# The seam from the first output product to gate-up: high parts first, low parts behind them, and the weight splits placed elsewhere

## The chip, the cores and the metric

The kernel runs on one core of one Trainium2 chip. Its engines are TensorE (PE in the profile, with its weight loads as PEld), VectorE (DVE), ScalarE (ACT), GpSimd (POOL) and SyncE (SP, which here only issues DMA transfers). The metric is the time of one execution in device microseconds. The kernel before took 1119.88 us as the median of three runs (1119.84 to 1121.58).

## The reference

Two transformer blocks on 512 tokens of 1024 features in fp32, one after the other. The change touches the place in the first block where attention ends and the feed-forward part begins:

```python
mixed = concatenate([rms_norm(out_a, group_norm_a), rms_norm(out_b, group_norm_b)], axis=-1) @ w_out
x = x + rms_norm(mixed, norm_mix_post)
h = rms_norm(x, norm_ffn_pre)
f = (silu(h @ w_gate) * (h @ w_up)) @ w_down
```

The product with w_out is called out1 in the kernel, the two products with w_gate and w_up are gate-up (gu1). Each of gate and up has 2816 columns, 22 tiles of 128. The second block has the same parts under the names out2 and gu2.

## The kernel before

**Layout and precision.** Features lie on the 128 partitions and tokens run along the free dimension, so x is eight blocks k of 128 features by 512 tokens (`xres[:, k, :]`). Each fp32 operand of a product is written as a high part in the format fp32r and a low part that holds what is left. A product is three matmuls: high weights by high state, high weights by low state, low weights by high state. The state h has the tiles `hh` (high) and `hl` (low); a chunk of weights, 1024 x 128, has `raw`, `wh` and `wl`, with a ring of four slots for chunks. The weights of gate-up tile j are chunk gu1+j. A split of a chunk is two steps: ACT copies `raw` to `wh` (`act_split`, L460), and DVE subtracts to get `wl` (`vec_split`, L472). ACT's step needs the slot's last tile to be multiplied, and DVE's step releases the load that SP issues into that slot of `raw`.

**Halves.** At this seam the tokens are taken in two halves of 256. The last three tiles of out1 are multiplied for the first half of the tokens and then for the second (units 5 to 7 and 8 to 10). From each half the kernel takes the mean square (ACT squares, DVE adds, PE sums over the partitions with a matrix of ones in `half_sum`, ACT makes `rstd` from it), and then, block by block: DVE scales (`vec_scale`, L1573, into `ta`), DVE adds to x (`vec_update`, L1580), ACT writes the high part of h (`act_half_h`, L1681) and a square for the next norm (L1682), and DVE writes the low part (`vec_half_low`, L1585). `vec_mix` and `vec_mix_add` (L1540, L1547) take a unit of out1 out of the banks, and `vec_half_square` (L1557) adds a square. The norm of h itself is not needed at this point, since its factor is applied to the products later.

**Gate-up's start.** `pe_gu1_first` multiplies the first four tiles of gate-up (two of gate, two of up), one per bank, for the first half of the tokens as blocks come ready, with the sum of squares of the second half (`half_sum(pe, 1, ...)`) put between; then for the second half. `pe_halves` (L1156 to L1158) does all three matmuls of a block and tile together and waits for the low part of the block. Then `pe_gate_up` goes on with tile 4, whose weights are in the slot of tile 0, by `products` (L551 to L553) for all 512 tokens; before it only `slot_wait` stands, a wait for the low split of chunk gu1+4.

**Order of work.** The order on each engine is written out by hand, and each engine takes its list in order. DVE's list at the seam is `vec_take1`, its last part `vec_second_half`, then `vec_sum_squares` and `vec_tokens`. In `vec_tokens` one sum of token blocks (L2182) stands ahead of the splits of chunks gu1+4 and gu1+5. ACT's list is `act_take1` and then `act_begin`: eight copies with gain (L2449), and then its steps of the same two splits. Waits are on semaphores. A scale counts up `scaled`, and the update waits for its own count:

```python
def vec_update(v, jn, k, half):
    n = HALVES[half]
    v.wait_ge(jn.scaled, KT * half + k + 1)
```

`vec_second_half` serves also the join behind the first down product (join2), where the second block's input begins.

Of the kernel before, what the change touches and what calls it, by code (L numbers as in the profile page):

```python
# [34 lines left out]
KT = D // P  # L35
# [11 lines left out]
RING = 4  # L47
# [17 lines left out]
HALVES = (slice(0, S // 2), slice(S // 2, S))  # L65
# [202 lines left out]
def build(nc, x_in, w_in, wpool_in, cols_in, mats_in, rope_in, out):  # L268
    ctx = ExitStack()
    with ctx:  # L270
# [872 lines left out]
        def pe_halves(pe, c0, t0, h, half, order):  # L1143


            n = HALVES[half]
            seen_k = -1
            for k, j in order:
                slot, bank = (c0 + j) % RING, banks[(t0 + j) % 4]
                first, last = (half, k) == (0, 0), (half, k) == (1, KT - 1)  # L1150
                if first:
                    slot_wait(pe, c0 + j)
                if k > seen_k:
                    pe.wait_ge(h.low, KT * half + k + 1)
                    seen_k = k
                pe.matmul(bank[:, n], wh[:, slot, k, :], hh[:, k, n], start=first, stop=False, skip_group_check=True)  # L1156
                pe.matmul(bank[:, n], wh[:, slot, k, :], hl[:, k, n], start=False, stop=False, skip_group_check=True)  # L1157
                ins = pe.matmul(bank[:, n], wl[:, slot, k, :], hh[:, k, n], start=False, stop=last, skip_group_check=True)  # L1158
                if last:
                    ins.then_inc(used, 1)  # L1160

        def pe_gu1_first(pe):

            c0, t0 = CHUNK0["gu1"], TILE0["gu1"]
            pe.wait_ge(bank_read, t0 - 1)
            pe_halves(pe, c0, t0, h_ffn1, 0, [(k, j) for k in range(2) for j in range(2)] + [(k, 2) for k in range(2)]
                      + [(k, j) for k in (2, 3) for j in range(3)])
            half_sum(pe, 1, banks[7])
            pe_halves(pe, c0, t0, h_ffn1, 0, [(k, j) for k in (4, 5, 6) for j in range(3)] + [(k, 3) for k in range(7)]
                      + [(7, j) for j in range(4)])  # L1170
            pe_halves(pe, c0, t0, h_ffn1, 1, [(k, j) for k in range(SPLIT) for j in range(4)]
                      + [(k, j) for j in range(4) for k in range(SPLIT, KT)])

# [396 lines left out]
        def vec_scale(v, jn, k, half):  # L1570

            n = HALVES[half]
            v.scalar_tensor_tensor(ta[:, k % 2, n], jn.mixed[:, k, n], col(jn.post, k), rstd[:, n], ALU.mult, ALU.mult)\  # L1573
                .then_inc(jn.scaled, 1)
# [4 lines that stand above are left out]
            v.wait_ge(x_loaded[k // 2], 32)  # L1579
            v.tensor_tensor(xres[:, k, n], xres[:, k, n], ta[:, k % 2, n], ALU.subtract if jn is join2 else ALU.add).then_inc(x_new, 1)  # L1580
# [12 lines left out]
        def vec_second_half(v, jn, ready):  # L1593

            v.wait_ge(ready, 1)
            for k in range(KT):
                vec_scale(v, jn, k, 1)
                if k == 0:
                    vec_half_low(v, jn, 7, 0)
                if k >= 2:  # L1600
                    vec_half_low(v, jn, k - 2, 1)
                vec_update(v, jn, k, 1)
            for k in (6, 7):
                vec_half_low(v, jn, k, 1)

        def vec_take1(v):

            c0, g0 = CHUNK0["out1"], CHUNK0["gu1"]
            v.wait_ge(n_ga.ready, 2)
            v.wait_ge(ln_b, 1)  # L1610
            v.tensor_tensor(sq[:, :], sq[:, :], rstd[:, :], ALU.subtract).then_inc(ln_ratio, 1)
            v.wait_ge(n_gb.ready, 1)
            for u in range(5):
                vec_mix(v, u)
                if u == 1:
                    v.wait_ge(n_mp.squared, 1)
                    v.tensor_tensor(acc[:, :], acc[:, :], sw[:, 0, :], ALU.add).then_inc(n_mp.added, 1)
                elif u > 1:
                    add_square(v, n_mp, u - 1, acc)
                vec_mix_add(v, u)  # L1620
                vec_split(v, c0 + u + RING)
            for u in (5, 6, 7):
                vec_mix(v, u)
                if u == 5:
                    add_square(v, n_mp, 4, acc)
                else:
                    vec_half_square(v, u - 1, 0)
                vec_mix_add(v, u)
            vec_mix(v, 8)
            vec_mix_add(v, 8)  # L1630
            v.wait_ge(n_mh[0].ready, 1)
            vec_scale(v, join1, 0, 0)
            vec_split(v, g0 + 1)
            vec_update(v, join1, 0, 0)
            vec_scale(v, join1, 1, 0)
            vec_mix(v, 9)
            vec_half_square(v, 5, 1)
            vec_update(v, join1, 1, 0)
            vec_mix_add(v, 9)
            for k in range(2, KT):  # L1640
                vec_scale(v, join1, k, 0)
                vec_half_low(v, join1, k - 2, 0)
                vec_update(v, join1, k, 0)
                if k == 3:
                    vec_split(v, g0 + 2)
                if k == 4:
                    vec_mix(v, 10)
                    vec_half_square(v, 6, 1)
                    vec_mix_add(v, 10)
            vec_split(v, g0 + 3)  # L1650
            vec_half_low(v, join1, 6, 0)
            vec_second_half(v, join1, n_mh[1].ready)

        def act_h(act, k, x_done, h, pre, norm, before=0):
# [29 lines left out]
        def act_take1(act):  # L1684
            c0, g0 = CHUNK0["out1"], CHUNK0["gu1"]
            for d in range(5):
                act_split(act, c0 + d + RING)
                act.wait_ge(bank_read, TILE0["out1"] + d + 1)
                act_square(act, n_mp, d, mixed1[:, d, :])
            for d in (5, 6, 7):  # L1690
                act_half_square(act, d, 0)
            act_half_rstd(act, n_mh[0], 0, banks[6], eps=False)
            act_split(act, g0 + 1)
            act_half_square(act, 5, 1)
            act_half_h(act, join1, 0, 0)
            act_split(act, g0 + 2)
            act_half_h(act, join1, 1, 0)
            act_half_square(act, 6, 1)
            act_half_h(act, join1, 2, 0)
            act_half_h(act, join1, 3, 0)  # L1700
            act_split(act, g0 + 3)
            act_half_h(act, join1, 4, 0)
            act_half_square(act, 7, 1)
            act_half_h(act, join1, 5, 0)
            act_half_h(act, join1, 6, 0)
            act_half_rstd(act, n_mh[1], 1, banks[7], eps=False)
            act_half_h(act, join1, 7, 0)
            for k in range(KT):
                act_half_h(act, join1, k, 1)

# [1250 lines left out]
```

## Time and profile before

| | |
|---|---|
| median of three runs (the three) | 1119.88 us (1119.84, 1119.88, 1121.58) |
| profiled execution, its own time | 1121.23 us |
| its span, first to last instruction | 1119.4 us |
| mean granted TensorE clock | 0.997 |
| PE busy | 1093.6 us (98% of the span) |
| PEld busy | 971.4 us (87%) |
| DVE busy | 831.7 us (74%) |
| ACT busy | 612.9 us (55%) |
| POOL busy | 120.8 us (11%) |
| chain of work that ended last | PE 89%, DVE 4%, ACT 3%, others 1% or less each |

Rows come from one profiled execution. Times in it are microseconds from the span's start. The busy time of PE counts pipelined matmuls that overlap, so the distance from the start of one matmul to the start of the next says more than the duration of one. In a timeline's row, brackets give how long the engine was idle before it and which instruction's end released it; x2 means two like instructions merged into one row. The profiled execution is not the median run: it lies 1.35 us above it.

### The profile page before, as it was taken

What the parts mean: (1) busy time and instruction counts of PE and PEld (TensorE: products, weight loads), DVE (VectorE), ACT (ScalarE), POOL (GpSimd) and SP (SyncE); (2) the same over time, 40 slices, a digit from 0 to 9 for tenths busy, and PEclk for the clock granted to TensorE, in tenths of its full rate; (3) what the DMA queues carried; (4) which work ended last, traced back from release to release, by engine and by line L of the source; (5) the groups of instructions that cost most, each with busy time, mean ns of one, the idle gap of its engine ahead of it and who ended that gap; (6) DMA issues with size and microseconds to landing.
All of it is one profiled execution on the core that took longest, in us unless ns stands there. A gap on an engine that the chain in (4) does not pass through costs nothing.

```text
span 1119.4 us, 18196 instructions
## 1 busy us (share of the span) xinstructions
PE 1093.6 (98%) x6848; PEld 971.4 (87%) x6848; DVE 831.7 (74%) x1425; ACT 612.9 (55%) x1109; POOL 120.8 (11%) x143
## 2 busy tenths in 40 slices
PE   8999989999999999999999999999999999999997
PEld 6688867999999999888898887787899999988886
DVE  6788886798989888733377878666699988885333
ACT  6787785476555555522255558545455555563231
POOL 1476644000000000000000004200000000000000
PEclk9999999999999999999999999999999999999999
DMA  7323322322333333433323220032233333333322
GB/s 283 108 75 88 84 57 91 112 64 90 115 98 95 113 114 114 124 106 110 112 67 114 77 79 34 19 96 60 91 113 110 95 99 114 114 132 111 96 57 76
DMA packets 34150, 109.30 MB, mean 98 GB/s; under 512 B 4368, under 2 KB 7056, under 8 KB 33936
## 3 DMA queue, kind: packets, MB, share of 16 engines
q1 hardware_dynamic: 33312, 107.22, 31.4%
q8 instruction: 55, 0.90, 0.3%
q10 hardware_dynamic: 752, 0.92, 0.3%
q14 instruction: 31, 0.25, 0.1%
HBM read 100.78 MB, written 2.10 MB: 92 GB/s over the span
## 4 chain that ended last, share of the span: by engine, by line
PE 89%; DVE 4%; ACT 3%; issue 1%; POOL 1%; DMA 1%; ACTq 0%; SPq 0%; DVEq 0%; POOLq 0%
PE bank L551 13%; PE bank L552 13%; PE bank L553 13%; PE bank L2121 11%; PE bank L2120 11%; PE bank L2119 11%; PE bank L1073 2%; PE bank L1083 2%; PE bank L1156 1%; PE bank L1028 1%; PE bank L1030 1%; PE bank L1029 1%; PE bank L1157 1%; PE bank L1158 1%; PE bank L2606 1%
## 5 line engine op out<-in xcount | busy, mean ns | idle before, releaser
L472 DVE TENSOR_TENSOR wl<-raw,wh 128x1024 fp32r<-128x1024 f32 x108 | 133.7, 1239 | 132.1 <-ACT wh L460 131.6
L460 ACT ACTIVATE wh<-raw 128x1024 fp32r<-128x1024 f32 (+1 forms) x109 | 114.0, 1049 | 165.3 <-PE bank L553 152.8
L2119 PE MATMUL bank<-h,wh 128*128 128x256 f32 x576 | 163.0, 283 | 0.0
L2120 PE MATMUL bank<-h,wh 128*128 128x256 f32 x576 | 163.0, 283 | 0.0
L2121 PE MATMUL bank<-h,wl 128*128 128x256 f32 x576 | 163.0, 283 | 0.0
L2121 PE MATMUL bank<-hh,wl 128*128 128x256 f32 x432 | 122.3, 283 | 0.0
L2120 PE MATMUL bank<-hl,wh 128*128 128x256 f32 x432 | 122.3, 283 | 0.0
L2119 PE MATMUL bank<-hh,wh 128*128 128x256 f32 x432 | 122.2, 283 | 0.0
L551 PE MATMUL bank<-gh,wh 128*128 128x512 f32 x308 | 119.8, 389 | 0.0
L552 PE MATMUL bank<-gl,wh 128*128 128x512 f32 x308 | 119.8, 389 | 0.0
L553 PE MATMUL bank<-gh,wl 128*128 128x512 f32 x308 | 119.8, 389 | 0.0
L551 PE MATMUL bank<-hh,wh 128*128 128x512 f32 x288 | 117.1, 407 | 2.2 <-DVE wl L472 1.4
L552 PE MATMUL bank<-hl,wh 128*128 128x512 f32 x288 | 112.7, 391 | 0.0
L553 PE MATMUL bank<-hh,wl 128*128 128x512 f32 x288 | 112.6, 391 | 0.0
L2119 PEld LDWEIGHTS bank<-h,wh 128*128 128x128 f32 x576 | 110.6, 192 | 0.0
L2120 PEld LDWEIGHTS bank<-h,wh 128*128 128x128 f32 x576 | 110.6, 192 | 0.0
L2121 PEld LDWEIGHTS bank<-h,wl 128*128 128x128 f32 x576 | 110.6, 192 | 0.0
L2119 PEld LDWEIGHTS bank<-hh,wh 128*128 128x128 f32 x432 | 82.9, 192 | 0.1
L2120 PEld LDWEIGHTS bank<-hl,wh 128*128 128x128 f32 x432 | 82.9, 192 | 0.1
L2121 PEld LDWEIGHTS bank<-hh,wl 128*128 128x128 f32 x432 | 82.9, 192 | 0.0
L2273 ACT ACTIVATE wh<-raw 128x512 fp32r<-128x512 f32 (+1 forms) x72 | 60.4, 844 | 40.8 <-PE bank L2121 40.7
L2481 ACT ACTIVATE ta<-ta 128x256 f32<-128x256 f32 x72 | 29.8, 414 | 89.8 <-DVE ta L2300 89.8
(303 smaller groups left out, 2657.6 us busy)
## 6 DMA issues: line engine op xcount, KB each, us to landing
raw<-weights SPq DMA_DIRECT2D x181, 512.0 KB, 3.7
xres<-x_t SPq DMA_DIRECT2D x8, 512.0 KB, 6.2
sw<-ta SPq DMA_DIRECT2D x36, 64.0 KB, 2.0
out_t<-final SPq DMA_DIRECT2D x6, 256.0 KB, 2.1
q<-sw SPq DMA_DIRECT2D x10, 128.0 KB, 2.3
q<-ta SPq DMA_DIRECT2D x10, 128.0 KB, 2.3
rope<-angles SPq DMA_DIRECT2D x1, 1024.0 KB, 10.3
sw<-ta ACTq DMA_DIRECT2D x4, 64.0 KB, 2.8
```

Of the source, the lines that this page charges most:

```text
L460: act.activation(wh[:, j, :, n], raw[:, j, :, n], ACT.Copy).then_inc(high_split, 1)
L472: v.tensor_tensor(wl[:, j, :, :], raw[:, j, :, :], wh[:, j, :, :].bitcast(F32), ALU.subtract)\
L551: pe.matmul(bank[:, :], wh[:, slot, b, :], ah[:, k, :], start=first and n == 0, stop=False)
L552: pe.matmul(bank[:, :], wh[:, slot, b, :], al[:, k, :], start=False, stop=False)
L553: ins = pe.matmul(bank[:, :], wl[:, slot, b, :], ah[:, k, :], start=False, stop=last and n == len(blocks) - 1)
L1073: ins = pe.matmul(dst, a, b, start=i == 0, stop=i == len(todo) - 1)
L1083: ins = pe.transpose(bank[:, q * P:(q + 1) * P], pr1[:, s % PR1, q, kb * P:(kb + 1) * P], ident[:, :])
L2119: pe.matmul(o, wh_half[:, h, k, :], high[:, k, :], start=first and k == 0, stop=False, skip_group_check=True)
L2120: pe.matmul(o, wh_half[:, h, k, :], low[:, k, :], start=False, stop=False, skip_group_check=True)
L2121: ins = pe.matmul(o, wl_half[:, h, k, :], high[:, k, :], start=False, stop=k == HK - 1, skip_group_check=True)
L2273: act.activation(high, src, ACT.Copy).then_inc(gu.unit_high.of, 1)
L2481: act.activation(t, t, ACT.Silu).then_inc(gu.taken.of, 1)
```

## The change

The first half of the first four gate-up tiles is multiplied in two passes. `pe_high_half` does, for each block and tile, the two matmuls with the high part of the state (by high and by low weights), and waits for high parts only. Blocks 0 to 5 of all four tiles stand ahead of the sum of squares of the second half, blocks 6 and 7 behind it. `pe_low_half` then does the matmuls of high weights with the low part, all blocks and tiles. The second half is as it was.

On DVE, the low parts of the first half move behind all eight updates, so that each scale is followed by its update; the low parts of the weights of tiles 2 and 3 (chunks gu1+2 and gu1+3) are made after blocks 1 and 3, and the last unit of out1 is taken after block 5. The low part of block 7 leaves `vec_second_half` for join1. On ACT, the high part of the weights of tile 3 comes ahead of blocks 2 and 3, the last square of out1 comes after block 5, and `rstd` of the second half comes after block 7.

```diff
--- before.py
+++ after.py
@@ -1159,15 +1159,40 @@
                 if last:
                     ins.then_inc(used, 1)
 
+        def pe_high_half(pe, c0, t0, h, order):
+
+            n = HALVES[0]
+            seen_k = -1
+            for k, j in order:
+                slot, bank = (c0 + j) % RING, banks[(t0 + j) % 4]
+                if k == 0:
+                    slot_wait(pe, c0 + j)
+                if k > seen_k:
+                    pe.wait_ge(h.high, k + 1)
+                    seen_k = k
+                pe.matmul(bank[:, n], wh[:, slot, k, :], hh[:, k, n], start=k == 0, stop=False, skip_group_check=True)
+                pe.matmul(bank[:, n], wl[:, slot, k, :], hh[:, k, n], start=False, stop=False, skip_group_check=True)
+
+        def pe_low_half(pe, c0, t0, h, order):
+
+            n = HALVES[0]
+            seen_k = -1
+            for k, j in order:
+                if k > seen_k:
+                    pe.wait_ge(h.low, k + 1)
+                    seen_k = k
+                pe.matmul(banks[(t0 + j) % 4][:, n], wh[:, (c0 + j) % RING, k, :], hl[:, k, n], start=False, stop=False, skip_group_check=True)
+
         def pe_gu1_first(pe):
 
             c0, t0 = CHUNK0["gu1"], TILE0["gu1"]
             pe.wait_ge(bank_read, t0 - 1)
-            pe_halves(pe, c0, t0, h_ffn1, 0, [(k, j) for k in range(2) for j in range(2)] + [(k, 2) for k in range(2)]
-                      + [(k, j) for k in (2, 3) for j in range(3)])
+            pe_high_half(pe, c0, t0, h_ffn1, [(k, j) for k in range(2) for j in range(2)] + [(k, 2) for k in range(2)]
+                         + [(k, j) for k in (2, 3) for j in range(3)] + [(k, 3) for k in range(4)]
+                         + [(k, j) for k in (4, 5) for j in range(4)])
             half_sum(pe, 1, banks[7])
-            pe_halves(pe, c0, t0, h_ffn1, 0, [(k, j) for k in (4, 5, 6) for j in range(3)] + [(k, 3) for k in range(7)]
-                      + [(7, j) for j in range(4)])
+            pe_high_half(pe, c0, t0, h_ffn1, [(k, j) for k in (6, 7) for j in range(4)])
+            pe_low_half(pe, c0, t0, h_ffn1, [(k, j) for k in range(KT) for j in range(4)])
             pe_halves(pe, c0, t0, h_ffn1, 1, [(k, j) for k in range(SPLIT) for j in range(4)]
                       + [(k, j) for j in range(4) for k in range(SPLIT, KT)])
 
@@ -1595,7 +1620,7 @@
             v.wait_ge(ready, 1)
             for k in range(KT):
                 vec_scale(v, jn, k, 1)
-                if k == 0:
+                if k == 0 and jn is join2:
                     vec_half_low(v, jn, 7, 0)
                 if k >= 2:
                     vec_half_low(v, jn, k - 2, 1)
@@ -1629,26 +1654,24 @@
             vec_mix(v, 8)
             vec_mix_add(v, 8)
             v.wait_ge(n_mh[0].ready, 1)
-            vec_scale(v, join1, 0, 0)
-            vec_split(v, g0 + 1)
-            vec_update(v, join1, 0, 0)
-            vec_scale(v, join1, 1, 0)
-            vec_mix(v, 9)
-            vec_half_square(v, 5, 1)
-            vec_update(v, join1, 1, 0)
-            vec_mix_add(v, 9)
-            for k in range(2, KT):
+            for k in range(KT):
                 vec_scale(v, join1, k, 0)
-                vec_half_low(v, join1, k - 2, 0)
                 vec_update(v, join1, k, 0)
+                if k == 0:
+                    vec_split(v, g0 + 1)
+                if k == 1:
+                    vec_mix(v, 9)
+                    vec_half_square(v, 5, 1)
+                    vec_mix_add(v, 9)
+                    vec_split(v, g0 + 2)
                 if k == 3:
-                    vec_split(v, g0 + 2)
-                if k == 4:
+                    vec_split(v, g0 + 3)
+                if k == 5:
                     vec_mix(v, 10)
                     vec_half_square(v, 6, 1)
                     vec_mix_add(v, 10)
-            vec_split(v, g0 + 3)
-            vec_half_low(v, join1, 6, 0)
+            for k in range(KT):
+                vec_half_low(v, join1, k, 0)
             vec_second_half(v, join1, n_mh[1].ready)
 
         def act_h(act, k, x_done, h, pre, norm, before=0):
@@ -1696,15 +1719,13 @@
             act_split(act, g0 + 2)
             act_half_h(act, join1, 1, 0)
             act_half_square(act, 6, 1)
-            act_half_h(act, join1, 2, 0)
-            act_half_h(act, join1, 3, 0)
             act_split(act, g0 + 3)
-            act_half_h(act, join1, 4, 0)
+            for k in (2, 3, 4, 5):
+                act_half_h(act, join1, k, 0)
             act_half_square(act, 7, 1)
-            act_half_h(act, join1, 5, 0)
-            act_half_h(act, join1, 6, 0)
+            for k in (6, 7):
+                act_half_h(act, join1, k, 0)
             act_half_rstd(act, n_mh[1], 1, banks[7], eps=False)
-            act_half_h(act, join1, 7, 0)
             for k in range(KT):
                 act_half_h(act, join1, k, 1)
 
```

## Rows read from the trace of the kernel before

**Rows 1.** The page: span, and its part 1

```profile
span 1119.4 us, 18196 instructions
...
PE 1093.6 (98%) x6848; PEld 971.4 (87%) x6848; DVE 831.7 (74%) x1425; ACT 612.9 (55%) x1109; POOL 120.8 (11%) x143
```

**Rows 2.** Windows: start:end length, busy (instructions) per engine, clock, DMA share, GB/s

```profile
213.50:245.00 31.50, 30.20 (x244) 29.47 (x243) 31.21 (x69) 23.73 (x54) 0.00 (x0) 1.00 0.18 51
245.10:268.00 22.90, 22.90 (x102) 18.61 (x101) 21.74 (x25) 17.09 (x24) 0.00 (x0) 1.00 0.39 114
```

**Rows 3.** Timeline, PE: start us, us, engine line op [idle before <-releaser]

```profile
219.06 0.28 PE L1156 MATMUL bank<-hh,wh 128*128 128x256 f32 x1
...
221.42 0.39 PE L1156 MATMUL bank<-hh,wh 128*128 128x256 f32 x1 [0.49 <-DVE wl L472]
...
224.34 0.38 PE L1156 MATMUL bank<-hh,wh 128*128 128x256 f32 x1 [0.80 <-DVE hl L1585]
...
225.52 0.59 PE L1139 MATMUL bank<-acc,ones 128*128 128x256 f32 x2
...
233.60 0.28 PE L1156 MATMUL bank<-hh,wh 128*128 128x256 f32 x1
...
245.12 0.40 PE L551 MATMUL bank<-hh,wh 128*128 128x512 f32 x1
```

**Rows 4.** The timeline, PE's weight loads (PEld) at the next tile

```profile
245.00 0.19 PEld L551 LDWEIGHTS bank<-hh,wh 128*128 128x128 f32 x1
```

**Rows 5.** The timeline, DVE

```profile
220.16 1.21 DVE L472 TENSOR_TENSOR wl<-raw,wh 128x1024 fp32r<-128x1024 f32 x1
...
224.54 0.48 DVE L1573 SCALAR_TENSOR_TENSOR ta<-mixed,cols,rstd 128x256 f32<-128x256 f32 x1
224.94 0.47 DVE L1585 SCALAR_TENSOR_TENSOR hl<-xres,cols,hh 128x256 fp32r<-128x256 f32 x1
225.34 0.41 DVE L1580 TENSOR_TENSOR xres<-xres,ta 128x256 f32<-128x256 f32 x1
225.67 0.47 DVE L1573 SCALAR_TENSOR_TENSOR ta<-mixed,cols,rstd 128x256 f32<-128x256 f32 x1
...
228.33 0.47 DVE L1573 SCALAR_TENSOR_TENSOR ta<-mixed,cols,rstd 128x256 f32<-128x256 f32 x1
...
229.46 0.47 DVE L1573 SCALAR_TENSOR_TENSOR ta<-mixed,cols,rstd 128x256 f32<-128x256 f32 x1
229.97 0.43 DVE L1580 TENSOR_TENSOR xres<-xres,ta 128x256 f32<-128x256 f32 x1
...
243.61 1.22 DVE L472 TENSOR_TENSOR wl<-raw,wh 128x1024 fp32r<-128x1024 f32 x1
```

**Rows 6.** The timeline, DVE, at the join behind the first down product

```profile
581.22 0.48 DVE L1573 SCALAR_TENSOR_TENSOR ta<-mixed,cols,rstd 128x256 f32<-128x256 f32 x1
581.73 0.42 DVE L1580 TENSOR_TENSOR xres<-xres,ta 128x256 f32<-128x256 f32 x1
```

**Rows 7.** The timeline, ACT

```profile
216.28 0.51 ACT L1681 ACTIVATE hh<-xres,cols 128x256 fp32r<-128x256 f32 x1 [1.35 <-DVE xres L1580]
216.70 0.40 ACT L1682 ACTIVATE sqs<-xres 128x256 f32<-128x256 f32 x1
...
226.58 0.39 ACT L1675 ACTIVATE rstd<-bank 128x256 f32<-128x256 f32 x1
227.00 0.42 ACT L1676 ACTIVATE rstd<-rstd 128x256 f32<-128x256 f32 x1
...
242.14 1.06 ACT L460 ACTIVATE wh<-raw 128x1024 fp32r<-128x1024 f32 x1 [0.93 <-PE bank L1158]
```

**Rows 8.** Windows of an earlier stretch, 38 to 44

```profile
38.00:40.00 2.00, 0.90 (x3) 0.53 (x4) 0.96 (x2) 1.11 (x3) 0.87 (x1) 0.99 0.01 4
40.00:42.00 2.00, 2.00 (x4) 0.88 (x4) 1.57 (x2) 2.00 (x4) 0.41 (x1) 0.50 0.41 102
42.00:44.00 2.00, 2.00 (x8) 1.57 (x7) 0.96 (x3) 1.95 (x5) 1.11 (x1) 0.66 0.53 86
```

## The prediction

> **What bounds the kernel now.** I read the page first. PE is busy for 1093.6 of the 1119.4 us [rows 1], so a seam is worth at most the time in which PE stands still there, and only if nothing else holds PE a little later. The timeline of PE over the seam shows two stalls, 0.49 us for a weight split and 0.80 us for a low part of the hidden state, both made by DVE, and also what they cost in full [rows 3]. The second half's 96 matmuls run from 233.60 to 245.12, so one 256-column matmul takes 0.12 us. Ahead of the half sum at 225.52 stand 36 matmuls since 219.06, worth 4.32 us, in 6.46 us: 2.14 us are lost to stalls. Between 225.52 and 233.60 stand 60 matmuls, 7.20 us, and the half sum, 0.88 us [rows 3]. More than 2.14 us can't be won here.
>
> Then I looked at who could refuse that gain. The windows view shows DVE busy for 31.21 of the 31.50 us from 213.5 to 245.0, more than PE (30.20), and ACT with room (23.73) [rows 2]. That is one unbroken chain of DVE instructions, started by an output product's end, and its last link is the split of chunk gu1+4 at 243.61, which ends at 244.83 [rows 5]. A split that ends at 221.37 released PE at 221.42, so 0.05 us lie between [rows 3, 5]. PE can thus load weights of tile 4 from 244.88 on, and it did at 245.00 [rows 4]. The reader is to see that the slack is 0.12 us. PE's stalls earlier in the seam are nearly free, because PE would otherwise have stood at tile 4.
>
> **The change, part by part.** PE: the first half has the same 96 matmuls in another order, 64 with the high part of the state and then 32 with the low part, each on weights already split. At 0.12 us each they cost what they did. What goes is the wait for lows: the pass now follows the highs.
>
> DVE: the same instructions in another order, eight lows behind all eight updates, and splits 2 and 3 ahead. I call the 128 features of one k a block. In the old order something stands between the scale of a block (it writes ta) and the update (which waits for that scale): the low of two blocks earlier, a split, or a mix. Scale to low takes 0.40 us, low to update 0.40, update to the next scale 0.33. Where nothing stands between, in block 1 of the second half, scale to update takes 0.51 [rows 5], and 0.51 again at another join [rows 6]. A direct pair so costs 0.11 us more than two instructions that don't depend on each other. The new order makes all eight pairs of the first half direct, and block 0 of the second half too, since its low moved ahead: nine pairs, 9 x 0.11 = 0.99 us. The bounds are nothing (if that block were an exception) and 0.99; both samples say 0.51, so I take 0.99.
>
> The Trainium skill, "VectorE: DVE Perf Modes", section "The DRAIN you can't avoid", speaks against that price: it says that chained DVE operations wait for the pipe in any case, and that "the semaphore costs nothing extra here". By it the DVE term would be 0 in place of 0.99 us; the two rows of 0.51 against 0.40 do not agree with it.
>
> Second half on DVE: it begins at 228.33, with one low of the first half left for after its first scale [rows 5]. With that low ahead and eight direct pairs it begins at 228.33 + 0.40 + 0.88 = 229.61. The eight lows fill the 3.20 us before, so low 0 starts at 226.41, update 7 at 226.08, and the last mixed piece of out1 (its add, ahead of two scales and updates of 0.84 each and a step of 0.33) at 224.40. The update of block 4 stands five steps earlier (three of 0.33, one of 0.51 and its own 0.33), at 222.57, and ends 0.41 later at 222.98.
>
> PE in between: the high of block 4 takes ACT 0.51 us [rows 7], so it is there by about 223.55. Up to there PE has 16 pairs of matmuls, 3.84 us from 219.06, so it stands 0.65 us in all, not 2.14. It begins its second half at 219.06 + 11.52 + 0.88 + 0.65 = 232.11. The second half's first low stands behind three scales and two updates, 2.08 us after 229.61, and ends at 232.17; PE gets it at 232.22, and later blocks come every 1.13 us against 1.44 us of matmuls per block. The second half ends at 243.74, 1.38 us sooner than before.
>
> The half sum comes after block 5, at 223.55 + 8 x 0.24 = 225.47, by which time the add at 224.40 and ACT's square of it are done, and ends at 226.35. The two steps of rstd took 0.84 us [rows 7]; ACT has the highs and squares of blocks 6 and 7 ahead of them (0.51 and 0.40 long), the last over at about 227.4, so rstd is there at 228.25. DVE asks at 229.61: 1.36 us of cover. If that cover goes, every microsecond beyond it is added to the end.
>
> The splits on ACT: that of chunk gu1+3 needs the end of the last output product, 219.06 and a matmul's 0.28 at the latest, and that of chunk gu1+2 the end of the one before, 24 matmuls or 2.88 us earlier. Each takes 1.06 us [rows 7], so they are done by 217.5 and 220.4. DVE comes to its own at about 218 and 220.9 (back from the update of block 4: one scale, then the split of 1.21 us, two direct blocks of 0.84, the other split). Each low split lets SP issue one 512 KB load sooner, by two microseconds and by more; the DMA engines are busy for 0.18 of this stretch and 0.39 of the next [rows 2], so I cost them at nothing. ACT's split of chunk gu1+4 began at 242.14 after 0.93 us of waiting for PE [rows 7]; with PE sooner and ACT's blocks 0.99 us later it begins at 242.20, well ahead of DVE.
>
> **The sum.** DVE reaches the split of chunk gu1+4 at 243.61 + 0.99 = 244.60, ends at 245.82, and PE loads at 245.87 in place of 245.00: **+0.87 us**. PE arrives at 243.74 and stands some 2.1 us there. Behind it PE is busy without a gap to 268.0, while DVE has 1.16 us of idle time in 22.90 in which it can catch up [rows 2], so the 0.87 us go through to the end one for one. The profiled execution took 1121.23 us (span 1119.4, 1.83 around it) and would take 1122.10; it lies 1.35 us above the median of the three runs, of which two stand at 1119.84 and 1119.88 and one at 1121.58. On the median: 1119.88 + 0.87 = **1120.75 us**. About 0.2% (2.24 us) is what a measurement of this kernel can tell from no change, so this is no change that can be told.
>
> **Rivals.** (a) *A direct pair costs nothing.* Then DVE's chain keeps its length, the load comes at 244.88, and the end moves by -0.12 us: 1119.76. For it: only two samples stand against it. Against: they agree to the hundredth. This is the result that the Trainium skill's section named above would give.
>
> (b) *The stalls are won, faster.* If tile 4 did not wait for DVE, PE would go on at 243.74: -1.38 us, 1118.50; with every stall gone -2.14, 1117.74. It decides from the point at which DVE's split ends before 243.6, which needs DVE's chain to be 1.2 us shorter. The stalls [rows 3] speak for it at first sight; 31.21 busy of 31.50 [rows 2] against it.
>
> (c) *The clock falls, slower.* PE stands 2.1 us at tile 4. Earlier, PE was busy for 0.90 of the two microseconds from 38 to 40, and the granted clock was then 0.50 (the 1.2 GHz level) for two microseconds and 0.66 in the mean of the next two [rows 8], a loss of 1.00 + 0.68 = 1.68 us. Here that gives +2.55: 1122.43. It decides as soon as the clock falls at all. Against: through the stalls of 0.49 and 0.80 us it stayed at 1.00, the 2.4 GHz level [rows 2, 3]; but 2.1 us in one piece is longer than those.
>
> (d) *The half sum is late.* DVE then stands at the second half's start. From 229.61 on it adds one for one; rstd 2 us later than I find would give +0.87 + 0.64: 1121.39. Against: 1.36 us of cover.
>
> **Chances and range.** Forecast 0.70 (own range 1120.3 to 1121.3: a pair at 0.06 to 0.16 us); (a) 0.07, (b) 0.08, (c) 0.10, (d) 0.05. Faster by over 0.2% (below 1117.64) takes more than (b)'s far end: 0.03. Slower (above 1122.12) is most of (c) and a run spread like the three shown: 0.11. The rest, 0.86, is within. The range takes in (a), (d) and (c) and leaves out (b): 1119.2 to 1122.5.
>
> **What would show it.** The profile after should show: stalls of PE inside the first half of under 1 us; lows of the first half in a row from 226.4; scale to update 0.51 us nine times; a wait of about 2 us of the load of L551 on DVE's split, near 245.9; granted clock 1.00 after it. Wrong if that wait is missing, if DVE's chain is not longer, or if DVE idles at rstd.

## The result, and the profile of the changed kernel

The changed kernel takes 1122.22 us as the median of 22 runs (1120.75 to 1123.33), the kernel before 1120.62 us in 22 runs (1119.64 to 1122.07). The ratio is 1.0013, with a 95% interval of 1.0007 to 1.0018. By the ratio that is 1.5 us slower: the interval does not hold 1, and all of it lies within the 0.2% that the prediction calls no change. The forecast was +0.87 us. The profiled execution took 1122.55 us; the first rows of its page stand beside [rows 1].

```profile
span 1120.7 us, 18196 instructions
...
PE 1095.4 (98%) x6848; PEld 973.3 (87%) x6848; DVE 832.7 (74%) x1425; ACT 612.9 (55%) x1109; POOL 121.2 (11%) x143
```

The work is the same, count for count. The timeline of PE at the seam answers to [rows 3] and [rows 4] (L1173 is the high pass, L1184 the low pass, L1156 the second half, L551 tile 4, L600 the sum of squares of h behind tile 4):

```profile
217.80 0.28 PE L1173 MATMUL bank<-hh,wh 128*128 128x256 f32 x1
...
219.58 0.39 PE L1173 MATMUL bank<-hh,wh 128*128 128x256 f32 x1 [0.17 <-ACT hh L1704]
...
224.42 0.59 PE L1139 MATMUL bank<-acc,ones 128*128 128x256 f32 x2
...
227.19 4.00 PE L1184 MATMUL bank<-hl,wh 128*128 128x256 f32 x32
231.10 0.38 PE L1156 MATMUL bank<-hh,wh 128*128 128x256 f32 x1
...
244.75 0.50 PE L551 MATMUL bank<-hh,wh 128*128 128x512 f32 x1 [1.87 <-DVE wl L472]
...
251.96 1.02 PE L600 MATMUL bank<-acc,ones 128*128 128x512 f32 x2
```

Here, and wherever two kernels are compared below, times count from the first gate-up matmul, which is at 219.06 before and at 217.80 after. The half sum comes at +6.62 behind 48 matmuls of 0.12 us, so PE stood 0.86 us in the first half, in pieces mostly too short for a bracket, and no longer 2.14. The second half begins at +13.30, where before it began at +14.54: 1.24 us sooner. Tile 4 begins at +26.95, where before it was +26.06: later. The 1.87 us in the brackets is where the gain went; they end with a weight split of DVE. The timeline of DVE answers to [rows 5]:

```profile
212.70 0.42 DVE L1572 TENSOR_TENSOR mixed<-bank,ta 128x256 f32<-128x256 f32 x1
213.04 0.48 DVE L1598 SCALAR_TENSOR_TENSOR ta<-mixed,cols,rstd 128x256 f32<-128x256 f32 x1
213.56 0.43 DVE L1605 TENSOR_TENSOR xres<-xres,ta 128x256 f32<-128x256 f32 x1
...
224.95 0.43 DVE L1605 TENSOR_TENSOR xres<-xres,ta 128x256 f32<-128x256 f32 x1
225.29 3.25 DVE L1610 SCALAR_TENSOR_TENSOR hl<-xres,cols,hh 128x256 fp32r<-128x256 f32 x8
228.46 0.48 DVE L1598 SCALAR_TENSOR_TENSOR ta<-mixed,cols,rstd 128x256 f32<-128x256 f32 x1
228.97 0.43 DVE L1605 TENSOR_TENSOR xres<-xres,ta 128x256 f32<-128x256 f32 x1
...
243.47 2.35 DVE L472 TENSOR_TENSOR wl<-raw,wh 128x1024 fp32r<-128x1024 f32 x2
```

A scale and its update are 0.52 us apart in the first pair shown and 0.51 in the second, where 0.40 was between two instructions that don't depend on each other [rows 5]. The stretch has one bracket, 0.18 us at 237.60 for ACT's last high part of the second half, and the kernel before has the same one at 237.73; otherwise DVE waits for nothing. Its chain from the add at 212.70 to the split at 243.47 takes 30.77 us. Before it took 29.65 (213.96 to 243.61), so it is 1.12 us longer. The statistic of the second half comes from ACT at 226.95 (timeline of ACT, beside [rows 7]); DVE asks for it at 228.46 and has 1.5 us of cover:

```profile
226.13 0.36 ACT L1698 ACTIVATE rstd<-bank 128x256 f32<-128x256 f32 x1
226.53 0.42 ACT L1699 ACTIVATE rstd<-rstd 128x256 f32<-128x256 f32 x1
```

The windows behind the wait show what the forecast had only as a rival (columns as in [rows 2]; the figure behind the five engines is the granted clock, here 1.00 twice, then 0.61, 0.50, 0.50 and 0.68):

```profile
243.00:245.00 2.00, 0.25 (x1) 0.26 (x2) 2.00 (x3) 2.00 (x6) 0.00 (x0) 1.00 0.00 0
245.00:246.00 1.00, 1.00 (x5) 0.79 (x5) 1.00 (x2) 1.00 (x3) 0.00 (x0) 1.00 0.26 86
246.00:247.00 1.00, 1.00 (x4) 0.85 (x3) 1.00 (x2) 1.00 (x2) 0.00 (x0) 0.61 0.93 348
247.00:248.00 1.00, 1.00 (x4) 0.71 (x3) 1.00 (x1) 0.12 (x1) 0.00 (x0) 0.50 1.11 213
248.00:249.00 1.00, 1.00 (x4) 0.81 (x3) 1.00 (x2) 0.87 (x1) 0.00 (x0) 0.50 0.77 311
249.00:250.00 1.00, 1.00 (x4) 0.77 (x4) 1.00 (x2) 1.00 (x2) 0.00 (x0) 0.68 0.22 90
```

PE is busy in every microsecond from 245 on, yet the granted clock is 0.50, the 1.2 GHz level, from 247 to 249, and 0.61 and 0.68 in the mean of the microsecond ahead of it and the one behind. The sum of squares of h comes at +34.16, where before it came at +31.53: 1.00 us of the 2.63 were there when tile 4's weights were loaded (+26.94 against +25.94), and 1.63 were lost to the clock.

The spans differ by 1.3 us. The seam starts 1.26 us sooner in the execution after; there the clock did not fall early in the kernel as it had [rows 8], and the window that had 0.50 has 1.00.

```profile
38.00:40.00 2.00, 0.92 (x3) 0.54 (x4) 0.95 (x2) 1.11 (x3) 0.88 (x1) 1.00 0.01 4
40.00:42.00 2.00, 2.00 (x8) 1.30 (x8) 1.58 (x2) 2.00 (x4) 0.39 (x1) 1.00 0.40 102
```

So the account of these two executions is -1.26 (not the change), +1.00 (DVE's longer chain), +1.63 (the clock at the seam): 1.37 against 1.3.

### The profile page after: what moved, and what is told of

Its sections match the earlier page's. It is cut to its first block, busy times and chain, and to the rows that moved or that the text cites. A ratio compares the mean times of both kernels' runs of the same rounds, so it can differ in the third digit from the quotient of the medians.

```text
span 1120.7 us, 18196 instructions
## 1 busy us (share of the span) xinstructions
PE 1095.4 (98%) x6848; PEld 973.3 (87%) x6848; DVE 832.7 (74%) x1425; ACT 612.9 (55%) x1109; POOL 121.2 (11%) x143
## 4 chain that ended last, share of the span: by engine, by line
PE 86%; DVE 7%; ACT 3%; issue 2%; DMA 1%; POOL 1%; ACTq 0%; SPq 0%; DVEq 0%
PE bank L551 13%; PE bank L552 13%; PE bank L553 13%; PE bank L2142 11%; PE bank L2141 11%; PE bank L2140 11%; PE bank L1083 2%; PE bank L1073 2%; DVE wl L472 1%; PE bank L1028 1%; PE bank L1029 1%; PE bank L1030 1%; PE bank L2627 1%; PE bank L2626 1%; PE bank L2625 1%
## 5 line engine op out<-in xcount | busy, mean ns | idle before, releaser
L551 PE MATMUL bank<-hh,wh 128*128 128x512 f32 x288 | 117.0, 406 | 3.4 <-DVE wl L472 3.3
L551 PE MATMUL bank<-gh,wh 128*128 128x512 f32 x308 | 119.8, 389 | 0.0
```

The source lines that it names most:

```text
L551: pe.matmul(bank[:, :], wh[:, slot, b, :], ah[:, k, :], start=first and n == 0, stop=False)
```

## The experiments

Theory: the end of the seam is set by DVE's chain, which nine direct pairs lengthen; PE's order is nearly free. Its rivals: a direct pair costs nothing; PE's lost order costs the time; the clock behind the wait costs it. A first table gives all runs. Each ratio is to the runs of before that ran beside that kernel. "Tile 4" is the start of its first matmul, and "second block" the first matmul behind PE's wait for the second block's input, both in us from the first gate-up matmul of the profiled execution.

| kernel | median us (runs) | ratio to before [95%] | tile 4 | second block |
|---|---|---|---|---|
| before | 1120.62 (22) | 1 | 26.06 | 356.43 |
| after | 1122.22 (22) | 1.0013 [1.0007, 1.0018] | 26.95 | 359.07 |
| e1_next_scale_between | 1120.70 (11) | 0.9999 [0.9990, 1.0008] | 25.82 | 356.31 |
| e2_split_early | 1121.96 (11) | 1.0010 [1.0001, 1.0019] | 24.91 | 357.86 |
| e3_before_split_early | 1123.57 (11) | 1.0023 [1.0014, 1.0032] | 26.05 | 359.02 |
| e4_filled_wait | 1121.69 (11) | 1.0008 [0.9999, 1.0016] | 26.93 | 357.41 |
| e5_lows_between | 1121.84 (11) | 1.0011 [1.0003, 1.0020] | 27.35 | 357.83 |
| e6_split_before_token_sum | 1120.75 (11) | 0.9999 [0.9990, 1.0008] | 24.67 | 356.30 |
| e7_sums_on_pool | 1124.85 (5) | 1.0035 [1.0023, 1.0048] | 26.19 | 359.97 |
| e8_before_sums_on_pool | 1124.11 (5) | 1.0033 [1.0020, 1.0045] | 26.18 | 359.95 |
| e9_kept_product_sooner | 1120.92 (11) | 1.0002 [0.9993, 1.0011] | 24.71 | 356.34 |
| e10_before_same_moves | 1122.22 (11) | 1.0010 [1.0001, 1.0019] | 26.06 | 357.10 |
| e11_less_dve_work | 1119.09 (11) | 0.9987 [0.9978, 0.9995] | 24.68 | 355.16 |
| e12_before_less_dve_work | 1120.10 (11) | 0.9998 [0.9989, 1.0007] | 26.06 | 356.44 |

The expectations give the second block by the last matmul ahead of the wait, which starts 1.2 us sooner in every kernel.

### The pairs taken apart: e1_next_scale_between

The scale of block k+1 goes between the scale and the update of block k. The scales then write two buffers by turns (`ta`, `tb`), and the last low of the first half goes back behind the second half's first scale.

```diff
+            vec_scale(v, join1, 0, 0)
             for k in range(KT):
-                vec_scale(v, join1, k, 0)
+                if k + 1 < KT:
+                    vec_scale(v, join1, k + 1, 0)
                 vec_update(v, join1, k, 0)
...
-            for k in range(KT):
+            for k in range(KT - 1):
                 vec_half_low(v, join1, k, 0)
```

> The kernel after, but each scale of the first half now has the next block's scale between it and its update (into a second buffer), and the last low of the first half goes back between the second half's first scale and update: no new direct pair is left. If a direct pair costs 0.11 to 0.12 us (forecast), DVE's chain is 1.0 to 1.1 us shorter: the weights of tile 4 load 25.8 to 25.9 us after the first gate-up matmul (25.94 before, 26.94 after), PE's wait there falls from 1.9 to about 0.9 us, and the time is that of the kernel before, within 0.3 us. If direct pairs cost nothing (rival a), the load stays at 26.9 and the time at that of the kernel after, 1.5 us above before.

The timeline of DVE in this kernel:

```profile
221.32 0.42 DVE L1609 TENSOR_TENSOR xres<-xres,ta 128x256 f32<-128x256 f32 x1
221.65 0.48 DVE L1602 SCALAR_TENSOR_TENSOR tb<-mixed,cols,rstd 128x256 f32<-128x256 f32 x1
222.05 0.42 DVE L1609 TENSOR_TENSOR xres<-xres,ta 128x256 f32<-128x256 f32 x1
...
224.45 2.86 DVE L1614 SCALAR_TENSOR_TENSOR hl<-xres,cols,hh 128x256 fp32r<-128x256 f32 x7
```

The same two instructions are 0.40 us apart when the update is that of another block. Tile 4 comes at +25.82 instead of +26.95, and the time is that of before. With the same order of PE, the loss is gone: the price of the direct pairs is shown, and the rival that they cost nothing falls. PE's new order alone is worth nothing here, since it still waits for the same split (timeline of PE):

```profile
243.78 0.50 PE L551 MATMUL bank<-hh,wh 128*128 128x512 f32 x1 [1.14 <-DVE wl L472]
```

### The split that PE waits for, made sooner: e2_split_early and e3_before_split_early

In the kernel after (e2) and in the kernel before (e3), the split of chunk gu1+4 goes ahead of the last three of the seven additions of the sum of squares on DVE and of the token sum behind them, and ahead of four of ACT's eight copies with gain.

```diff
@@ vec_sum_squares, behind its first four additions
+            if jn is join1:
+                vec_split(v, CHUNK0["gu1"] + RING)
@@ vec_tokens
             vec_token(v, gu, "d1")
             if not late:
-                vec_split(v, c4)
                 vec_split(v, c4 + 1)
@@ act_begin
             act_tokens(act, gu, gain, "11")
+            if not late:
+                act_split(act, c4)
             act_tokens(act, gu, gain, "12")
             if not late:
-                act_split(act, c4)
                 act_split(act, c4 + 1)
```

> The kernel after, with the split of chunk gu1+4 sooner: on ACT behind the first four of its eight copies, on DVE behind the first four sums of squares, four instructions sooner. If that split alone holds tile 4 (forecast), PE goes from the second half into tile 4 without a wait, the load comes about 24.6 us after the first gate-up matmul, the clock has no reason to fall there, and the time is 1.2 to 1.4 us below before (ratio 0.9988). If the stall only moves on, to the sum of squares of h or to the split of chunk gu1+5, PE waits there instead and the time stays at or above that of before.

> The kernel before, with the same sooner split of chunk gu1+4 and nothing else. If PE in the kernel before was held by its stalls ahead and the split was ready 0.12 us before it was wanted (forecast), the sooner split wins nothing: load at 25.9 us after the first gate-up matmul, time within 0.2 us of before. If the sooner split is itself the gain, whatever PE's order is, the load comes about a microsecond sooner and the time falls by 1 us or more.

Both expectations missed. In e2 PE goes through tile 4 without a wait, at +24.91, 2.04 us sooner than after. But two waits appear 27 us later, in the first group of gate-up tiles that is made with seven products in place of eight (timeline of PE in e2; `acc` and `rh` are what ACT keeps of two of these products):

```profile
270.94 0.39 PE L2142 MATMUL bank<-h,wh 128*128 128x256 f32 x1 [1.22 <-ACT acc L2484]
...
274.64 0.38 PE L2142 MATMUL bank<-h,wh 128*128 128x256 f32 x1 [0.57 <-ACT rh L2490]
```

At the second block e2 stands 1.21 us ahead of after and 1.43 us behind before; as after had lost 1.63 us to the clock by then, nothing of the 2.04 us is left. In e3 the move itself stops DVE, because ACT has not yet made `wh`, the step ahead of DVE's (timeline of DVE in e3):

```profile
244.15 1.23 DVE L472 TENSOR_TENSOR wl<-raw,wh 128x1024 fp32r<-128x1024 f32 x1 [2.60 <-ACT wh L460]
```

Tile 4 stays at +26.05, PE gets the same two waits of 1.24 and 0.57 us in the group, and the time is 1.0023. In neither kernel is DVE's list shorter: DVE comes to the token sums behind its split of chunk gu1+5 at +28.37 in e2 and at +29.51 in e3, where it was +26.85 before and +27.95 after. So what e2 wins for PE at tile 4 is asked back where PE next needs DVE and ACT.

### The wait filled: e4_filled_wait

Four matmuls of the ones matrix by four blocks of `hh`, whose result nobody reads, stand ahead of tile 4, so that PE is busy while it waits.

```diff
             pe_gu1_first(pe)
+            for i in range(4):
+                pe.matmul(banks[6][:, HALVES[0]], ones[:, :], hh[:, i, HALVES[0]].bitcast(F32), start=i == 0, stop=i == 3)
             pe_gate_up(pe, gu1, n_fp, 7)
```

> The kernel after, with four fp32 matmuls of 256 columns (1.7 us, into a bank that is free there, results unused) put ahead of tile 4, so that PE works during most of its wait. If the kernel after loses 1.0 us by DVE's chain and the rest by the clock that falls after the wait, the load stays near 26.9 us after the first gate-up matmul, the granted clock stays at 1.00 behind it, the sum of squares of h comes 5.6 us after the load and not 7.2, and the time is about 1.0 us above before, at or below that of the kernel after. If the clock has no part, the time is that of the kernel after, about 1.5 us above before, or higher.

The timeline of PE, with the fp32 matmuls as two instructions each, and one window of the whole stretch:

```profile
245.10 1.89 PE L2866 MATMUL bank<-hh,ones 128*128 128x256 f32 x8
247.12 0.50 PE L551 MATMUL bank<-hh,wh 128*128 128x512 f32 x1
...
252.70 1.02 PE L600 MATMUL bank<-acc,ones 128*128 128x512 f32 x2
```

```profile
240.00:260.00 20.00, 19.86 (x107) 16.73 (x107) 19.01 (x22) 17.16 (x29) 0.00 (x0) 1.00 0.25 79
```

Tile 4 is as late as after (+26.93), the granted clock stays at 1.00, and L600 comes 5.58 us behind tile 4 instead of 7.21. At the second block this execution stands 0.98 us behind before: DVE's part alone. The median lies between those of before and after, but its interval reaches from 0.9999 to 1.0016, so the timed runs do not separate it from either, and that the clock stays up with the wait filled is shown by this one execution.

### Lows between again: e5_lows_between

PE as after; on DVE each low stands between the scale and the update two blocks later, as before.

```diff
                 vec_scale(v, join1, k, 0)
+                if k >= 2:
+                    vec_half_low(v, join1, k - 2, 0)
                 vec_update(v, join1, k, 0)
...
-            for k in range(KT):
-                vec_half_low(v, join1, k, 0)
+            vec_half_low(v, join1, 6, 0)
```

> The kernel after, but with each low of the first half back between the scale and the update of two blocks later, as in the kernel before; PE's two passes and the places of the splits stay. Forecast: what counts is that nothing stands between scale and update, not which instruction does, so DVE's chain is as short as in the kernel before: tile 4 starts 25.8 us after the first gate-up matmul (26.06 before, 26.95 after) and the first seven-product group 48.6 us after it (48.74 before). Time within 0.3 us of before. If the lows in one row are what costs, this gives the same; if the splits moved ahead are what costs, tile 4 stays at 26.9.

The chain should have been short again and was not. With lows between them the updates come later, so the highs, the half sum (+7.59 instead of +6.62) and rstd come later, and DVE stands (timeline of DVE):

```profile
230.30 0.48 DVE L1598 SCALAR_TENSOR_TENSOR ta<-mixed,cols,rstd 128x256 f32<-128x256 f32 x1 [1.21 <-ACT rstd L1700]
```

This is rival (d) of the prediction, in a kernel where the cover of 1.5 us is gone. Seven of the nine pairs are apart here. By an estimate of 0.11 us for each, that saves 0.77 of the 1.21 us, so that DVE comes 0.44 us later than after; tile 4 is 0.40 us later. Lows behind updates are what gives that cover; e1 keeps them there and takes only the pairs apart.

### The same split ahead of one token sum: e6_split_before_token_sum

On top of e1, DVE's split of chunk gu1+4 goes ahead of the sum of token blocks that stood before it (1.14 us from start to start); ACT's order stays.

```diff
+            if not late:
+                vec_split(v, c4)
             vec_token(v, gu, "d1")
             if not late:
-                vec_split(v, c4)
                 vec_split(v, c4 + 1)
```

> No direct pairs (next block's scale between), and DVE's split of chunk gu1+4 one instruction sooner, ahead of the first sum of token blocks (1.14 us), when ACT's step is already done. DVE does not idle for it. Theory that DVE's chain bounds the whole stretch up to the first group: tile 4 starts at 24.7 to 24.9 and the group is wanted at 47.5, but DVE's chain has kept its length, so PE waits again in the group for 0.2 to 0.6 us and the time is 0.5 to 0.9 us below before (ratio 0.9993). If the split alone is the gate: 1.2 us below before and no wait in the group.

Tile 4 comes at +24.67 and the first group of seven products 1.27 us sooner than before. At the second block 0.13 us of it is left. Part of it goes in a wait in the group (timeline of PE):

```profile
273.86 0.39 PE L2146 MATMUL bank<-h,wh 128*128 128x256 f32 x1 [0.56 <-ACT rh L2496]
```

The median does not differ from before.

### Sums of squares on GpSimd: e7_sums_on_pool and e8_before_sums_on_pool

The seven additions of the sum of squares of h (4.3 us of DVE) go to GpSimd, on top of e1 (e7) and of before (e8).

```diff
-            vec_sum_squares(v, join1)
@@ block.gpsimd
                 gpsimd_tick(g, t)
+            vec_sum_squares(g, join1)
             gpsimd_attention2(g)
```

> No direct pairs, and the seven sums of squares of h (4.5 us on DVE) done by GpSimd, which is idle here and takes 1.29 us for such an add, 9 us in all, ready some 28.5 us after the first gate-up matmul against 30.3 wanted. DVE then waits for ACT's copies instead: tile 4 starts at 24.7 to 24.9 us and DVE stays about 1.1 us ahead of the kernel before up to the group. If DVE's chain is the bound: no wait of PE at tile 4 and in the group, time 1.1 to 1.3 us below before (ratio 0.9989). If something else bounds, or GpSimd slows DVE, the group comes no sooner than 48.7.

> The kernel before, with the seven sums of squares of h on GpSimd and nothing else. PE's stalls in the first half stay as they were, so a shorter chain on DVE behind them wins nothing: tile 4 at 26.05 us, group at 48.7 us, time within 0.2 us of before. If DVE's chain alone is the bound, whatever PE's order is, this gains as much as the kernel with both, 1.1 us or more.

Both missed, by far: 0.35% and 0.33% slower. The timelines of DVE and of GpSimd in e7:

```profile
241.00 1.66 DVE L2209 TENSOR_TENSOR h_raw<-h_raw 128x1024 f32<-128x1024 f32 x1 [3.10 <-ACT h_raw L2476]
242.58 4.53 DVE L472 TENSOR_TENSOR wl<-raw,wh 128x1024 fp32r<-128x1024 f32 x2
247.03 5.67 DVE L2209 TENSOR_TENSOR h_raw<-h_raw 128x1024 f32<-128x1024 f32 x3
252.63 1.21 DVE L472 TENSOR_TENSOR wl<-raw,wh 128x1024 fp32r<-128x1024 f32 x1
```

```profile
237.76 6.03 POOL L1743 TENSOR_TENSOR sqs<-sqs 128x512 f32<-128x512 f32 x4 [55.77 <-ACT sqs L1711]
243.76 4.50 POOL L1746 TENSOR_TENSOR sqs<-sqs 128x512 f32<-128x512 f32 x2
248.34 2.15 POOL L1748 TENSOR_TENSOR acc<-sqs 128x512 f32<-128x512 f32 x1
```

While GpSimd adds, DVE needs 4.53 us for two splits (2.35 in the kernel after) and 5.67 for three token sums (3.49 there); behind GpSimd's last addition a split takes 1.21 again. The work left DVE's list and stayed in its time: DVE first stands 3.10 us for ACT's copies, and then its own instructions take longer.

### ACT's kept product sooner: e9_kept_product_sooner and e10_before_same_moves

The wait of e6 ends with an ACT instruction that keeps a product (`act_u1`). Here it stands one step sooner in ACT's list, on top of e6 (e9). In e10, before gets this move and that of e6.

```diff
             act_unit(act, gu, 1, "12")
+            act_u1(act, gu, 0)
             act_unit(act, gu, 0, "22")
             act_group_silu(act, gu, 0, 0)
-            act_u1(act, gu, 0)
```

> The kernel with no direct pairs and the split of chunk gu1+4 one instruction sooner, and in the first group of both blocks ACT takes the product P6 out of its bank (act_u1) between its two splits of weights, not behind a silu that waits for DVE. If the wait of 0.56 us that was left in the group came from that place in ACT's list, it goes: tile 4 at 24.7 us, group at 47.5, the next sevens without a wait, and the seam stays 1.2 us ahead of the kernel before: time 1.0 to 1.3 us below it (ratio 0.999). If DVE's chain bounds there too, a wait of about 0.5 us stays under another name and the time is 0.5 us below before.

> The kernel before, with the two last moves alone (DVE's split of chunk gu1+4 ahead of the first sum of token blocks, act_u1 sooner), without the change's two passes. Forecast: PE's stalls in the first half stay, PE comes to tile 4 no sooner than the split did, so tile 4 at 26.0 us, group at 48.7, time within 0.2 us of before. If the moves alone are the gain: 1 us below before.

The wait for `rh` is gone, and another stands in its place (timeline of PE in e9):

```profile
277.78 0.35 PE L2147 MATMUL bank<-h,wh 128*128 128x256 f32 x1 [0.47 <-DVE wl L2309]
```

It ends with DVE, and the time is still that of before. ACT's name in the wait before was that of the last link; that DVE's work is behind it is tested next. In e10 PE has a like wait of 0.43 us, and the kernel is slower than before (1.0010), which its forecast did not have. Its second block comes 0.67 us later than before; 0.43 us of that is this wait, and the rest was not traced.

### Less work for DVE: e11_less_dve_work and e12_before_less_dve_work

If DVE's amount of work takes back what e6 wins, less work must let it through. For the first four hidden tiles of the first block, DVE makes the low part for 64 of 512 tokens only, and the down product takes the high part in its place, so that PE has the same matmuls. Both kernels leave out the correction that these low parts give, so only their time says something. It is on top of e6 in e11, on before in e12.

```diff
-            v.tensor_tensor(gl[:, f, :], hidden_source(f), gh[:, f, :].bitcast(F32), ALU.subtract)...
+            n = slice(0, 64) if gu is gu1 and f < PLAIN else slice(0, S)
+            v.tensor_tensor(gl[:, f, n], hidden_source(f)[:, n], gh[:, f, n].bitcast(F32), ALU.subtract)...
```

> No direct pairs and DVE's split of chunk gu1+4 ahead of the first sum of token blocks, and DVE does less in gate-up's start: the low parts of the first four hidden tiles of the first block are made for 64 of 512 tokens only (the down product takes the high part in their place, with as many matmuls). That saves DVE about 0.45 us four times, 1.8 us in all. If DVE's chain is what gives the seam's gain back in the first groups, less work on DVE keeps it: tile 4 at 24.7 us after the first gate-up matmul, group at 47.5, no wait of PE of over 0.3 us in the groups, the second block's input 1.0 us or more sooner than in the kernel before (its first wait there begins at 355.2), time 0.8 to 1.2 us below before (ratio 0.999). If something else gives it back, the second block's input comes at 355.1 as in the kernel with the full work.

> The kernel before with the same lighter work on DVE, the low parts of the first four hidden tiles for 64 tokens only, the high part in their place. Forecast: with the old order PE's stalls stay, tile 4 at 26.05 us, and PE is behind DVE in the groups anyway, so the second block's input comes at 355.2 as before and the time is within 0.2 us of before. If less work on DVE is a gain by itself, this too is 1 us below before.

e11 is faster than before, 0.9987 [0.9978, 0.9995]; e12 is not, 0.9998 [0.9989, 1.0007]. The rows at the second block's input, first e11 (gate-up began at 217.89), then e12 (at 217.85):

```profile
573.05 0.39 PE L1156 MATMUL bank<-hh,wh 128*128 128x256 f32 x1 [0.93 <-DVE hl L1614]
```

```profile
574.29 0.38 PE L1156 MATMUL bank<-hh,wh 128*128 128x256 f32 x1 [0.93 <-DVE hl L1585]
```

That is +355.16 against +356.44 and, before, +356.43. The 1.27 us that e6 had at the group now reach the second block. It takes both: PE's order with the short chain to win time at tile 4, and less work on DVE behind it to keep it.

## Why the prediction was right, and where its sizes were off

**The stalls of PE were nearly free: right.** PE stood 0.86 us in the first half (0.65 forecast), began its second half 1.24 us sooner (1.38) and stood at tile 4 for 1.87 us by the matmuls and 2.07 by the weight loads (2.1). e1 has the same order of PE, and its time is that of before.

**DVE's chain sets the seam: right; its term was 1.12 us, not 0.99.** The weights of tile 4 were loaded 1.00 us later, as 1.12 less the slack of 0.12; the forecast had 0.87, as 0.99 less 0.12. The pairs measured 0.51 and 0.52. Summed over the rows, the steps that begin with a scale are 1.05 us longer than before, and the rest is hundredths: 0.06 over the sixteen steps behind updates, 0.04 over those behind lows. The chain is DVE's but for one link, the 0.18 us behind ACT's last high, which both kernels have and the prediction did not mention.

**The step that was mis-sized is the clock.** The prediction gave rival (c) a chance of 0.10, on the ground that the clock had stayed at 1.00 through stalls of 0.49 and 0.80 us. In the profiled execution the clock fell behind the wait, and cost 1.63 us (1.68 forecast for that rival). That the wait brought it on there is what e4 speaks for: with PE kept busy in it, the clock stayed up. A wait of about this length does not do it every time: in e7 the clock stayed at 1.00 behind a wait of 1.50 us at tile 4 and behind one of 1.82 us in the first group of seven products (timeline of PE in e7), and in e8 behind one of 1.80.

```profile
244.93 0.50 PE L551 MATMUL bank<-hh,wh 128*128 128x512 f32 x1 [1.50 <-DVE wl L472]
...
272.70 0.39 PE L2146 MATMUL bank<-h,wh 128*128 128x256 f32 x1 [1.82 <-ACT acc L2489]
```

How often it falls is not shown by a trace, since only one execution of each kernel has one. The fourteen traces show it falling at three places while PE works: between 40 and 46 (before, e3, e4, e5, e6, e10), between 146 and 154 (after, e2, e4, e6, e7, e9) and behind tile 4 (after alone). The four traces without a fall (e1, e8, e11, e12) have a mean granted clock of 0.998 or 0.999.

So the mean of an execution gives a hint. Of the 96 executions of before that ran beside the experiments, 28 have 0.998, and take 1120.06 us on average; of the 22 of after, 5 have 0.998 and take 1120.89. These differ by 0.83 us, close to the forecast. The other executions of after take 1121.46 to 1123.33. The measured +1.5 us is then about 0.8 to 1.0 us of DVE's chain, and the rest a clock that falls behind tile 4 in some executions; the split between the two is argued from these groups and not shown, and by the averages of the 22 runs in place of the medians the whole is 1.2 us.

**Luck in the range.** The forecast's own range was +0.4 to +1.4 us, and the measured +1.5 lies just above it. The median of 1122.22 us lies within the whole range near its upper end, which was there for rival (c), and the median of before itself stands at 1120.62 in 22 runs and not at the 1119.88 of three from which the range was counted.

**The other rivals.** (a) A direct pair that costs nothing: fell with e1 and with the rows of the kernel after. (b) The stalls won: not in this kernel, as DVE's chain is 30.77 us long. The kernels e2 and e6 bring tile 4 forward to +24.91 and +24.67, as (b) wanted, and are not faster; the prediction did not see that the stretch behind tile 4 would take the gain back as well. It reasoned that DVE has 1.16 us of idle time up to 268 in which to catch up, and stopped there. (d) The half sum late: not in the kernel after, with 1.5 us of cover (1.36 forecast), and seen in e5.

**The early splits and loads** were costed at nothing. No wait of PE or DVE for them stands in the seam after.

## What to carry to other kernels

When PE is 98% busy and a second engine runs without a gap beside it, follow that engine's chain to the next place where PE must have its result, before valuing PE's stalls: a stall won ahead of that place can be given back there, as here. Where one engine's list has an instruction right behind the one that it depends on, put an independent one between; here, with DVE, that was worth as much as the whole change cost (e1). A wait that is gathered into one piece may cost more than the same time in small pieces, because the clock can fall behind it, as it did in the profiled execution of after and did not in those of e7 and e8.

## What the runs showed of the hardware

On DVE, an update of 128x256 that waits for the scale right in front of it started 0.51 to 0.52 us behind that scale (after). Where it waited for an earlier scale, it started 0.40 us behind the one in front (e1).

The granted clock fell behind a wait of PE of 1.87 us (0.61, then 0.50 for two microseconds, then 0.68). It was 1.00 behind waits of 1.14 us in e1, 0.99 in e5, 1.50 and 1.82 in e7 and 1.80 in e8. The same kind of gap does not always do it: with PE busy for 0.90 us of the two from 38 to 40 it fell in the execution of before [rows 8], and with 0.92 us it stayed in that of after.

GpSimd and DVE slow each other on fp32 tensor additions and subtractions: a 128x1024 split took 2.27 us instead of 1.17 (half of 4.53, half of 2.35), and GpSimd's 128x512 additions 1.5 to 2.25 us, where others of that size took 1.29 earlier in the trace of e7. The Trainium skill, "SBUF — State Buffer", section "SBUF: two separate sides", says that a VectorE instruction with two inputs in SBUF and a GpSimd instruction that reads SBUF lock each other out for a whole instruction. The rows agree that they hold each other up; that it is a whole instruction each time, they don't show.
